# Summing the first two modulation parts on TensorE in float32, in place of VectorE, ScalarE and GpSimd

## The reference, cut to what matters

```python
def modulation(cond, w, b):
    return jnp.split(jax.nn.silu(cond) @ w + b, 6, axis=-1)

sh1, sc1, g1, sh2, sc2, g2 = modulation(cond_lat, ada_w[i], ada_b[i])
u = modulate(h, sh1, sc1)                    # layer_norm(h) * (1 + sc1) + sh1
mc = modulation(cond_ctx, ada_w[i], ada_b[i])
uc = modulate(hc, mc[0], mc[1])              # the 256 context tokens, first layer only
```

## Time and profile before

| what | value |
|---|---|
| median of 3 runs | 3623.73 us (3623.05 to 3628.56) |
| time of the profiled execution | 3624.9 us |
| its span | 3623.0 us |
| PE busy | 3290.0 us, 91% |
| DVE, ACT, POOL busy | 1891.0, 1161.5, 482.9 us |
| mean granted TensorE clock | 0.959 |

### The profile page before, as it was taken

One profiled execution on the slowest core, in us unless ns is written; L12 is line 12 of the kernel. 1 busy time (PEld: TensorE's weight loads), 2 busy tenths in 40 slices (PEclk: granted clock), 3 DMA queues, 4 the chain that ended last, 5 costly groups with the idle time before them and its releaser, 6 DMA issues.

```text
span 3623.0 us, 37255 instructions
## 1 busy us (share of the span) xinstructions
PE 3290.0 (91%) x15207; PEld 2739.4 (76%) x15207; DVE 1891.0 (52%) x2635; ACT 1161.5 (32%) x1709; POOL 482.9 (13%) x289
## 2 busy tenths in 40 slices
PE   2999887879999999869799999997996899999997
PEld 2788776667888888667588888886874778888886
DVE  5625577564555554675544444446776643333335
ACT  5311587252212112342522111125355431212222
POOL 4001464030000000322000000012480000000000
PEclk9999999889999999889899999998997999999998
DMA  6435211202333332011121111110120111111111
GB/s 194 140 104 181 79 53 33 99 18 70 103 95 93 93 95 69 26 47 35 41 59 47 52 47 47 47 47 25 36 89 18 47 47 47 47 55 57 52 47 47
DMA packets 190996, 237.98 MB, mean 66 GB/s; under 512 B 9671, under 2 KB 149562, under 8 KB 190826
## 3 DMA queue, kind: packets, MB, share of 16 engines
q1 hardware_dynamic: 180250, 198.07, 18.1%
q0 software_dynamic: 9136, 32.28, 2.4%
q10 hardware_dynamic: 1440, 5.24, 0.5%
HBM read 218.74 MB, written 16.83 MB: 65 GB/s over the span
## 4 chain that ended last, share of the span: by engine, by line
PE 75%; DVE 13%; ACT 8%; issue 3%; DMA 1%; POOL 0%; SPq 0%; DVEq 0%; ACTq 0%; POOLq 0%
PE psum L522 24%; PE psum L523 24%; PE psum L524 24%; DVE small L642 2%; ACT temp L825 2%; DVE small L1284 1%; DVE H L1389 1%; ACT U_hi L528 1%; DVE PT_lo L533 1%; ACT prob L1250 1%; DVE small L667 1%; DVE split L533 1%; PE psum L588 1%; ACT split L528 1%; PE psum L815 1%
## 5 line engine op out<-in xcount | busy, mean ns | idle before, releaser
L522 PE MATMUL psum<-U_hi,split 128*128 128x512 f32 x2108 | 836.0, 397 | 60.3 <-DVE split L533 36.0
L523 PE MATMUL psum<-U_lo,split 128*128 128x512 f32 x2108 | 830.1, 394 | 0.0
L524 PE MATMUL psum<-U_hi,split 128*128 128x512 f32 x2108 | 828.9, 393 | 0.0
L528 ACT CAST split<-raw 128x1024 fp32r<-128x1024 f32 x260 | 266.4, 1044 | 1260.2 <-PE psum L524 875.7
L522 PE MATMUL psum<-split,A_hi 128*128 128x512 f32 x1536 | 600.5, 391 | 3.0 <-ACT temp L825 3.0
L523 PE MATMUL psum<-split,A_hi 128*128 128x512 f32 x1536 | 599.7, 390 | 0.0
L524 PE MATMUL psum<-split,A_lo 128*128 128x512 f32 x1536 | 599.5, 390 | 0.0
L1389 DVE TENSOR_TENSOR H<-H,psum 128x512 f32<-128x512 f32 x416 | 281.4, 686 | 592.2 <-PE psum L524 592.2
L522 PEld LDWEIGHTS psum<-U_hi,split 128*128 128x128 f32 x2108 | 401.8, 191 | 152.6 <-DVE split L533 37.2
L533 DVE TENSOR_TENSOR split<-raw,split 128x1024 fp32r<-128x1024 f32 x260 | 324.5, 1263 | 282.5 <-ACT split L528 279.6
L524 PEld LDWEIGHTS psum<-U_hi,split 128*128 128x128 f32 x2108 | 401.5, 190 | 85.1
(11 more groups left out here) (320 smaller groups left out, 3807.8 us busy)
## 6 DMA issues: line engine op xcount, KB each, us to landing
raw<-in_mlp_w_dram SPq DMA_DIRECT2D x128, 512.0 KB, 4.4
raw<-in_ada_w_dram SPq DMA_DIRECT2D x96, 512.0 KB, 4.3
raw<-in_w_in_dram SPq DMA_DIRECT2D x38, 512.0 KB, 3.9
raw<-in_w_up_dram SPq DMA_DIRECT2D x32, 512.0 KB, 4.1
raw<-in_w_down_dram SPq DMA_DIRECT2D x32, 512.0 KB, 4.3
H<-in_x_dram ACTq DMA_DIRECT2D x8, 512.0 KB, 4.7
raw<-d_q SPq DMA_DIRECT2D x32, 128.0 KB, 2.8
raw<-d_k SPq DMA_DIRECT2D x16, 256.0 KB, 3.9
```

The costliest lines, as they stand in the source:

```text
L522: pe.matmul(out, l_hi, r_hi, start=start, stop=False)
L523: pe.matmul(out, l_hi, r_lo, start=False, stop=False)
L524: return pe.matmul(out, l_lo, r_hi, start=False, stop=stop)
L528: return act.copy(hi, src).then_inc(*k.hi.inc(*key))
```

## The change

In place of the two accumulators there is one matmul pair for each unit: the stationary operand is `cc[:, i, :]`, 128 x 2, so that both conditions are summed at once, and the moving operand is one half (512 columns) of the unit as it has landed, in plain float32. Eight units accumulate in two PSUM banks, of which two partitions are used. VectorE copies the two rows to SBUF in halves, TensorE turns them by eight transposes of 2 x 128 into columns, and VectorE adds the bias as before. The next unit of `raw` is now released by TensorE alone (`ada_taken`). All ScalarE scalings (L751, L756) and all GpSimd additions (L707) of the stage go, and with them the VectorE sums (L574, L577) of these 16 units. The hats stand one behind the other. TensorE turns part 1 after the second unit of part 0, and for this waits for VectorE's copies, which stand behind the eighth hat.

```diff
 def pe_start(k, pe, on):
...
+    on.wait_ge(*k.cc_ok.at())
     for n, part in enumerate((1, 0)):
-        pe_ada_sum(k, pe, on, 0, part, (k.ada_x[:, n, :], k.ada_c[:, n, :]))
+        banks = [k.banks.take(on, ("ada row", part, half), (k.ada_row_ok, (part, half))) for half in range(2)]
+        for i in range(KT):
+            u = k.units[n * KT + i]
+            on.wait_ge(*k.landed(u))
+            for half in range(2):
+                m = pe.matmul(k.psum[0:2, banks[half], :], k.cc[:, i, :], u.raw[:, half * CH:(half + 1) * CH],
+                              start=i == 0, stop=i == KT - 1)
+            m.then_inc(*k.ada_taken.inc(0, part, i))
+            if (n, i) == (1, 1):
+                pe_turn_ada_rows(k, pe, on, 1)
+    pe_turn_ada_rows(k, pe, on, 0)
+
+def pe_turn_ada_rows(k, pe, on, part):
+    b = k.banks.take(on, ("ada", 0, part), (k.mod_ok, (0, part)))
+    for i in range(KT):
+        on.wait_ge(*k.ada_row_ok.at(part, i // 4))
+        m = pe.transpose(k.psum[:, b, 2 * i:2 * i + 2], k.ada_rows[0:2, part, i * P:(i + 1) * P], k.ident[0:2, 0:2])
+    m.then_inc(*k.ada_summed.inc(0, part))
...
 def act_start(k, act, on):
...
-    (hat(0), then the 16 units scaled for GpSimd with the other hats between them)
+    for t in range(TT + CTT):
+        hat(t)
     for s in range(2):
         act_weights(k, act, on, s)
...
 def dve_start(k, dve, on):
...
-    (hat(0), then dve_ada for the 16 units with the other hats between them)
+    def mod(part):
+        on.wait_ge(*k.ada_taken.at(0, part, KT - 1))
+        for half in range(2):
+            dve.tensor_copy(k.ada_rows[0:2, part, half * CH:(half + 1) * CH],
+                            k.bank("ada row", part, half)[0:2, :]).then_inc(*k.ada_row_ok.inc(part, half))
+
+    for t in range(TT + CTT):
+        hat(t)
+        if t == TT - 1:
+            mod(1)
+    dve_mod(k, dve, on, 0, 1, 2)
+    mod(0)
     dve_mod(k, dve, on, 0, 0, 2)
```

More of the change, by code:

```diff
@@ L245, in allocate @@
         self.ctx_raw = place("ctx_raw", r_at + 8 * KB, [P, CTT, D])
-        self.ada_x = place("ada_x", r_at + 16 * KB, [P, 2, UNIT])
-        self.ada_c = place("ada_c", r_at + 24 * KB, [P, 2, UNIT])
+        self.ada_rows = place("ada_rows", r_at + 16 * KB, [P, 2, UNIT])
         self.conv_in = place("conv_in", r_at + 16 * KB, [P, 4, T])
@@ L291, in allocate @@
         self.up_done, self.down_done = s("up_done"), s("down_done")
-        self.gate_turned, self.pe_done = s("gate_turned"), s("pe_done")
+        self.gate_turned, self.pe_done, self.ada_taken = s("gate_turned"), s("pe_done"), s("ada_taken")
         self.cc_ok, self.rooted, self.hat_ok = s("cc_ok"), s("rooted"), s("hat_ok")
-        self.ctx_scaled, self.taken, self.hi = s("ctx_scaled"), s("taken"), s("hi")
+        self.taken, self.hi = s("taken"), s("hi")
         self.relu_done, self.gate_ok, self.exp_done = s("relu_done"), s("gate_ok"), s("exp_done")
         self.act_done, self.normed = s("act_done"), s("normed")
+        self.ada_row_ok = s("ada_row_ok")
         self.consts_ok, self.cols_ok, self.lam_ok = s("consts_ok"), s("cols_ok"), s("lam_ok")
@@ L304, in allocate @@
         self.dve_gained = s("dve_gained")
-        self.ident_ok, self.ctx_added, self.pool_gained = s("ident_ok"), s("ctx_added"), s("pool_gained")
+        self.ident_ok, self.pool_gained = s("ident_ok"), s("pool_gained")
         self.pool_step, self.pool_done, self.att_lo = s("pool_step"), s("pool_done"), s("att_lo")
@@ L494, in free_raw @@
         if u.ada:
-            on.wait_ge(*self.ada_x_ok.at(*u.ada))
-            if u.ada[:2] in ((0, 1), (0, 0)):
-                on.wait_ge(*self.ctx_scaled.at(*u.ada))
+            on.wait_ge(*(self.ada_taken if u.ada[:2] in ((0, 1), (0, 0)) else self.ada_x_ok).at(*u.ada))
         else:
@@ L577, in dve_ada, with pe_ada_sum @@
         dve.scalar_tensor_tensor(acc, u.raw[:], c, acc, ALU.mult, ALU.add).then_inc(*k.ada_x_ok.inc(layer, part, i))
-def pe_ada_sum(k, pe, on, layer, part, accs):
+def pe_ada_sum(k, pe, on, layer, part, acc):
     on.wait_ge(*k.ada_x_ok.at(layer, part, KT - 1))
     on.wait_ge(*k.consts_ok.at())
-    if len(accs) > 1:
-        on.wait_ge(*k.ctx_added.at(part, KT - 1, 1))
     b = k.banks.take(on, ("ada", layer, part), (k.mod_ok, (layer, part)))
[L586 to L589, removed]
+    for i in range(KT):
+        m = pe.matmul(k.psum[:, b, i:i + 1], acc[:, i * P:(i + 1) * P], k.ones[:, 0:1], start=True, stop=True)
     m.then_inc(*k.ada_summed.inc(layer, part))
@@ L595, in dve_mod @@
     on.wait_ge(*k.cols_ok.at(1))
-    ps = k.bank("ada", layer, part)
+    ps = k.bank("ada", layer, part)[:, 0:conds * KT].rearrange("p (i a) -> p a i", a=conds)
     bias = k.columns("ada_b", 48 * layer + KT * part, KT)
@@ L599, in dve_mod @@
     for cond, mod in enumerate((k.mod[:, layer], k.mod_ctx)[:conds]):
-        m = dve.scalar_tensor_tensor(mod[:, KT * part:KT * part + KT], ps[:, KT * cond:KT * cond + KT], one, bias,
+        m = dve.scalar_tensor_tensor(mod[:, KT * part:KT * part + KT], ps[:, cond], one, bias,
                                      ALU.add, ALU.add)
@@ L697, in pool_start @@
                    k.a["lambda_qk"][0].rearrange("a d -> (a d)").partition_broadcast(P)).then_inc(*k.lambda_in.inc())
[L698 to L707, removed]
 def token_tile(k, t):
@@ L892, in pe_project @@
         if h == HEADS - 1:
-            pe_ada_sum(k, pe, on, 0, 2, (k.row_g,))
+            pe_ada_sum(k, pe, on, 0, 2, k.row_g)
     V = [k.unit("v", i) for i in range(4)]
@@ L917, in pe_project @@
             if m in (2, 6):
-                pe_ada_sum(k, pe, on, 0, 3 + m // 6, ((k.row_b, k.row_g)[m // 6],))
-    pe_ada_sum(k, pe, on, 0, 5, (k.row_b,))
+                pe_ada_sum(k, pe, on, 0, 3 + m // 6, (k.row_b, k.row_g)[m // 6])
+    pe_ada_sum(k, pe, on, 0, 5, k.row_b)
     pe_gate_row(k, pe, on, 0, 0)
@@ L1679, in pe_mlp @@
             if name == "mlp0" and 2 <= blk and tt == 0:
-                pe_ada_sum(k, pe, on, 1, blk - 2, ((k.row_g, k.row_b)[blk % 2],))
+                pe_ada_sum(k, pe, on, 1, blk - 2, (k.row_g, k.row_b)[blk % 2])
             pe_down_tile(k, pe, on, stage, tt, downs, lambda j, tt: a_operands(k, j, tt),
```

2 lines of the change are left out of this document (removed).

## The result

The changed kernel took 3603.38 us, median of 4 (3603.14 to 3603.76), the kernel before 3624.57 beside it; the ratio is 0.994 with a 95% interval of 0.9925 to 0.9955. That is 21.2 us less. The forecast was 3600 against 3623.73, 23.4 less, with a range of 3593 to 3613.

The account below looks back on a forecast made before the run. The first stage's own work, not its transfers, was taken as the bound. Last unit at 51 plus a 4.7 us chain start the context's first modulation at 55.7, not 79.1: 23.4 us gained, 3600.3 against 3623.73; range 3593 to 3613.

Parts of the forecast that it names:

- What bounds it, and that everything behind moves along: First stage: bound by its own work, not transfers; later TensorE-bound stages move one for one with the context's first modulation.
- The price of a unit: New matmuls on TensorE: 0.45 us a record, 1.82 us a unit at full clock, bounds 0.91 and 4.74.
- the slower rival: TensorE's units: weight loads in the open at half clock, 4.74 us a unit, 3640 us; chance 0.04.
- The clock: TensorE in the first stage: half clock for two units (3.41 us each), then full clock and staying up.
- the rival was right for one gap: TensorE stays at half clock through the first stage, 3.41 us a unit, gain 4.9, 3619 us; chance 0.08.
- The new wait: TensorE at part 1's transposes after unit 9: VectorE's copies 3.7 us early, the eight transposes cost 1 us.
- The last unit: End of unit 15 on TensorE: scheduled at 53 us, taken as 51.
- the bandwidth sum of 44.3: First stage's 20 transfers through by 15.1 + 10.5 MB / 360 GB/s = 44.3 us, by bandwidth alone.
- The chain behind it: From unit 15's end to the context's first modulation: copies 1.5, transposes 0.8, context transposes 2.0; 4.7 us taken.
- Hidden casts: ScalarE's casts of weight units 0 and 1, ahead of the context's first modulation: done by 54.5, hidden by 1 us.
- late hat: Tiles lose against units, part 1's copies come late, TensorE waits at unit 10; 3619 us; chance 0.03.
- given back: After the first stage: gain lost later, in the clock or at a formerly hidden transfer; 3624 us; chance 0.04.

Follow-up runs that it names:

- half_columns: The changed kernel, but from each part's second unit on only the first 256 of each 512 columns are summed; 3600.61 us.
- twice: The changed kernel with each of its new matmuls issued twice into the same sum; 3620.97 us.
- own_ring16: The changed kernel, but all 16 modulation units have a buffer of their own and are issued at once, three w_in units behind them; 3599.26 us.
- own_ring6: The changed kernel, but the 16 modulation units have six buffers of their own and the w_in units use the ring of three; 3600.96 us.
- ctx_on_pe: The changed kernel with only the context condition taken from TensorE's rows; VectorE sums the latent one as in the kernel before; 3609.89 us.
- c_on_pe: The changed kernel with only the latent condition taken from TensorE's rows; ScalarE and GpSimd sum the context one as in the kernel before; 3621.12 us.

## Why the prediction was right, point by point

*What bounds it, and that everything behind moves along.* Right: 21.21 us at the stage's end, 21.21 at the first wide matmul, 21.19 in the median. The distance from L911 to the first L520 is 9.51 us (forecast: unchanged at 9.5).

*The price of a unit.* Forecast 0.45 us a record and 1.82 a unit, worked out from a 128-column row that has no 512-column neighbour. Measured 0.43 a record and 1.73 a unit where units follow without a gap, 5% under the forecast; one unit alone takes 1.88 from first start to last end. So each column is streamed twice, as the prediction read it from the 128-column row. The weight load of two columns is short and hidden:

```profile
L683 PEld LDWEIGHTS psum<-raw,cc x64: 80/84/129, 11.2 to 52.7; 128*2 128x2 f32 x64
L683 PE MATMUL psum<-raw,cc x64: 591/592/1061, 11.2 to 53.2; 128*2 128x512 f32 x64
```

The upper bound of 4.74 us took a load of 128 columns for it, and was far off. With that the slower rival had nothing under it.

*The clock.* Forecast: two units at the lower level, then up and stay up. It rose sooner (three units in 7.69 us, of which the first took 3.59) and fell once, behind the one gap of 2.92 us, with unit 7 at half clock: 1.5 us lost (5.06 us for two units, against 3.61). So the rule of the Trainium skill, "TensorE: Matmul & The Clock Gate", section "HAM oscillation", that a burst behind a long transfer wait starts at half clock, is seen here behind that gap, and not behind the shorter ones of 0.2 to 1.8 us. In `half_columns`, where the bursts are half as long between the same transfers, the clock was at 0.71 to 0.73. So the rival was right for one gap of the ten, and its price for the whole stage (`twice`) was not paid.

*The new wait.* Forecast: copies 3.7 us early. The eighth hat ended at 35.9 (forecast 34.6), the copies at 38.2, TensorE came at 40.6: 2.4 us early. The rival named late tiles as its trigger. It needs none: in `own_ring16` the eighth hat ended at 34.9, 1 us sooner than in the change, and TensorE, fed faster, still waited 4.92 us.

*The last unit.* This is the term that was mis-sized. The schedule in the text came to 53, and I took 51, leaning on the bandwidth sum of 44.3. The last unit ended at 53.75. The bandwidth sum does not apply to a ring of three: landings took 6.1 us for units and 7.3 for tiles where I had some 6 for both, and the transfers came near 360 GB/s only from 20 to 35 us. Three stretches of the kernel after:

```profile
12.00:15.00 3.00, 3.00 (x5) 0.52 (x4) 2.54 (x8) 2.02 (x3) 0.00 (x0) 1.00 0.15 60
...
20.00:25.00 5.00, 3.24 (x8) 0.42 (x6) 2.04 (x8) 1.92 (x4) 0.00 (x0) 1.00 0.97 348
...
35.00:40.00 5.00, 4.81 (x10) 0.72 (x9) 3.23 (x9) 1.83 (x3) 0.00 (x0) 0.85 0.57 187
```

At the start all three buffers were full and waited for TensorE at half clock, and after 35 us units alone went round (187 to 256 GB/s). The step-by-step schedule should have been kept. Its rate of 2.1 us a unit for the last six was right: from unit 9's end at 40.66 to 53.75 they took 2.2 each, transposes included. Its present latency of 4.4 stands in no row; the earlier trace rows has 4.6, which makes no difference that counts.

*The chain behind it.* Forecast 4.7, measured 4.13: copies 1.29, transposes 0.40, the context's transposes 1.90, which ran at full clock, and 0.5 for the last cast and the steps between engines. Hidden casts: forecast to be through 1 us early, measured not hidden, by 0.4 us at most.

*The sum.* Forecast 23.4, measured 21.2: the last unit 2.75 later than taken, the chain 0.6 shorter.

*The chances.* They don't add up as written: clock, late hat and given back make 0.15, so "same" should have been 0.15 and not 0.13, and "faster" 0.81 and not 0.83.

## What to carry to other kernels

When one engine replaces three in a stage that streams weights, ask first what the loads can do: here removing 25 us of VectorE work and 40 of GpSimd work left a stage whose length is the round trip of three buffers, and 11 us more lay in depth plus the order of eight small transposes. A wait that is free in one version (copies behind the eighth hat) becomes the bound as soon as its engine is fed better, so change both together. On TensorE such a wait can cost twice its length, because the clock falls behind it: 2.49 us of waiting were worth 5.4 in `own_ring6`. Where your own schedule and a bandwidth bound disagree, the schedule with its latencies is the forecast and the bandwidth only its lower end.

## What the runs showed of the hardware

VectorE's sums and GpSimd's additions slowed each other. The sum took 1.711 us in the mean and the addition 1.446 in the kernel before. In `ctx_on_pe`, with GpSimd idle, and in `c_on_pe`, with VectorE free of sums:

```profile
L578 DVE SCALAR_TENSOR_TENSOR ada_acc<-raw,cc,ada_acc 128x1024 f32<-128x1024 f32 x14 | 18.0, 1284 | 3.2 <-DMA raw<-in_ada_w_dram 2.5 <-issue 0.3
```

```profile
L729 POOL TENSOR_TENSOR ada_acc<-ada_acc,temp 128x512 f32<-128x512 f32 x28 | 34.8, 1265 | 28.5 <-ACT temp L778 28.5
```

That is 14 x 0.43 = 6.0 us of VectorE's path and 28 x 0.18 = 5.1 of GpSimd's that only the neighbour cost. Single sums of the kernel before say the same, the first beside an addition (GpSimd at work from 27.92 to 34.02 and again from 34.78), the second with GpSimd idle but for its first 0.06 us:

```profile
32.74 2.37 DVE L577 SCALAR_TENSOR_TENSOR ada_x<-raw,cc,ada_x 128x1024 f32<-128x1024 f32 x1
...
41.86 1.27 DVE L577 SCALAR_TENSOR_TENSOR ada_x<-raw,cc,ada_x 128x1024 f32<-128x1024 f32 x1
```

ScalarE's scalings were not slowed: 0.709 us before, 0.710 in `c_on_pe`.

The granted clock printed for a stretch can be 1.00 where the spacing of records says half: until TensorE's first change of clock the rows of the kernel before showed 1.00, with transposes 0.21 us apart that are 0.11 apart at full clock:

```profile
75.53:78.84 3.31, 3.31 (x18) 3.31 (x19) 2.50 (x4) 0.00 (x0) 0.00 (x0) 1.00 0.13 34
```

And a TensorE with less work between the same transfers ran slower per column: in `half_columns` half the columns of a unit took 1.87 us at half clock, where the whole unit takes 1.88 at full clock.
